# Prompt attention from transposed scores: halves stacked on partitions, V beside ones as the stationary operand, maxima from a sweep of their own

## The chip, the cores and the metric

One core of one Trainium2 chip runs the whole program in one launch. The metric is the device time in microseconds, the median of the runs.

## The reference, cut to what matters

One step of a two-layer decoder: a chunked gMLP layer, then an attention layer with forgetting (decay by cumulated log-forget values), for a prompt of 1024 tokens and for 8 single tokens with 512 cached positions each. All is computed in fp32; here only the attention of the prompt changes, per head (16 heads of 64 values) over causal pairs of query and key.

```python
logits = jnp.einsum('nqhd,nkhd->nhqk', q, k).astype(jnp.float32) * (FA_HEAD_DIM ** -0.5)
decay = jnp.swapaxes(c_q, 1, 2)[..., :, None] - jnp.swapaxes(c_k, 1, 2)[..., None, :]
causal = k_pos[None, :] <= q_pos[:, None]
logits = jnp.where(causal, logits + decay, -jnp.inf)
p = jax.nn.softmax(logits, axis=-1)
return jnp.einsum('nhqk,nkhd->nqhd', p.astype(v.dtype), v)
# then, in the mixer
return (o * jax.nn.silu(z)) @ w_out + b_out
```

## The kernel before

Each fp32 product is done as three matmuls of fp32r parts: an operand is split into a high part (rounded to fp32r) and a low part (the rest), and `three` (L1345 to L1349) accumulates low*high, high*low and high*high. Token data lie transposed: features on the partitions, tokens on the free axis.

The program has stages: the modulation, 16 V blocks, 16 pairs of Z and U blocks, 8 output blocks of the first layer, its layer norm, then the stage around the change, 8 output blocks of the attention layer (L1644 to L1676), and the tail with the decode attention and the last layer norm.

The stage around the change is a loop of 8 phases, j = 0 to 7. Phase j does the attention of heads 2j and 2j+1, and, woven in, the projections of K, Q, V and Z for pair j+1: 4 blocks (q = 0 to 3) of 16 `step`s (L1522). A step is three matmuls of 512 columns; step 0 of each block also issues the narrow group `sample_cols` (L1501), 16 matmuls of 9 columns. Phases 1 to 6 are a hardware loop of two phases per turn, phase 7 has no projections any more.

In a phase before, i runs over 16 pairs (query tile qt = i // 2, head h = i % 2). For each, TensorE does `scores` (queries on the partitions, keys on the columns, K=64 rows of one head, three matmuls per up to 512 keys, and a mask matmul on the diagonal tile), VectorE adds the decay and takes the row's maximum in one custom operation (`logits`, L1165), ScalarE takes the exponential and its sum (`exp`, L725), TensorE transposes the probabilities tile by tile (`transpose_p`, L1578), ScalarE and VectorE split them (`pt_high` L719, `pt_low` L1172), and TensorE multiplies them with V (`values`, L1588 and L1590: probabilities stationary, V moving, 128 and 64 columns). `o_part` and `o_full` divide by the sum, eight transposes (L1633) bring the result back to features on partitions, and `gate_o` (L1189) multiplies by the gate z.

Each engine has its own program, an order written out by hand; they meet at semaphores. What a phase issues and when is in `phase` of each engine. Queues: SP issues the weight loads (`load_b`), GpSimd issues the loads of the decay rows (`load_c`) and the stores of k and v (`store_kv`), and in the last phase the cache pages for the decode attention. There, VectorE also does the first 11 of 32 decode `score`s (L1140, two operations of 1024 columns each), and ScalarE and VectorE split the first two rows of the attention's result (`y2_high`, `y2_low`). K and Q of a pair are kept twice (`par`), so that the next pair is split while the current is in use.

PSUM has 8 banks: 0 and 1 for the projections, 2 and 3 (`pair(1)`) for scores, 4 and 5 (`pair(2)`) for transposes, 6 and 7 for the result of the two heads.

## Time and profile before

| | us |
|---|---|
| median of 3 runs | 2042.86 (2042.25 to 2048.98) |
| span of the profiled execution | 2045.0 (no time of its own beside the span is listed) |
| TensorE busy | 1950.4 (95%) |
| VectorE busy | 876.2 (43%) |
| ScalarE busy | 587.6 (29%) |
| GpSimd busy | 189.3 (9%) |
| mean granted TensorE clock | 0.944 |

Busy is the union of an engine's instructions. In rows of single matmuls the duration contains the pipeline's depth, so two neighbours overlap; what one costs in a dense stream is the distance between starts. PEld is TensorE's weight load, which runs beside the matmul before it. The granted clock is a share of 2.4 GHz; 0.50 is 1.2 GHz. "idle <-X" names what the engine waited for, as inferred from semaphores.

### The profile page before, as it was taken

What the parts mean: (1) busy time and instruction counts of PE and PEld (TensorE: products, weight loads), DVE (VectorE), ACT (ScalarE), POOL (GpSimd) and SP (SyncE); (2) the same over time, 40 slices, a digit from 0 to 9 for tenths busy, and PEclk for the clock granted to TensorE, in tenths of its full rate; (3) what the DMA queues carried; (4) which work ended last, traced back from release to release, by engine and by line L of the source; (5) the groups of instructions that cost most, each with busy time, mean ns of one, the idle gap of its engine ahead of it and who ended that gap; (6) DMA issues with size and microseconds to landing.
All of it is one profiled execution on the core that took longest, in us unless ns stands there. A gap on an engine that the chain in (4) does not pass through costs nothing.

```text
span 2045.0 us, 29265 instructions
## 1 busy us (share of the span) xinstructions
PE 1950.4 (95%) x11208; PEld 1685.4 (82%) x11208; DVE 876.2 (43%) x1645; ACT 587.6 (29%) x1106; POOL 189.3 (9%) x215
## 2 busy tenths in 40 slices
...
DMA packets 44071, 164.23 MB, mean 80 GB/s; under 512 B 5610, under 2 KB 6250, under 8 KB 42818
## 3 DMA queue, kind: packets, MB, share of 16 engines
q1 hardware_dynamic: 26642, 103.52, 14.4%
...
q14 instruction: 34, 0.28, 0.0%
...
## 4 chain that ended last, share of the span: by engine, by line
PE 87%; DVE 6%; issue 3%; ACT 2%; DMA 1%; POOL 0%; POOLq 0%; SPq 0%; DVEq 0%; ACTq 0%
PE bank L1347 19%; PE bank L1349 18%; PE bank L1348 18%; PE bank L1578 4%; PE bank L1588 3%; PE bank L1559 3%; PE bank L1698 3%; PE bank L1446 3%; PE bank L1504 3%; PE bank L1590 2%; PE bank L1560 2%; PE bank L1561 2%; PE bank L1435 1%; PE bank L1356 1%; PE bank L1562 1%
## 5 line engine op out<-in xcount | busy, mean ns | idle before, releaser
L1347 PE MATMUL bank<-h_hi,w_lo 128*128 128x344 f32 x1152 | 373.7, 324 | 5.7 <-DVE h_lo L859 5.0
L1348 PE MATMUL bank<-h_lo,w_hi 128*128 128x344 f32 x1152 | 368.3, 320 | 0.0
L1349 PE MATMUL bank<-h_hi,w_hi 128*128 128x344 f32 x1152 | 368.0, 319 | 0.0
L1347 PE MATMUL bank<-x_hi,w_lo 128*128 128x512 f32 x528 | 228.6, 433 | 1.8 <-DVE kqvzS L1087 1.4
L1347 PEld LDWEIGHTS bank<-h_hi,w_lo 128*128 128x128 f32 x1152 | 217.2, 189 | 11.9 <-issue 9.7
L1348 PEld LDWEIGHTS bank<-h_lo,w_hi 128*128 128x128 f32 x1152 | 217.4, 189 | 0.0
L1349 PEld LDWEIGHTS bank<-h_hi,w_hi 128*128 128x128 f32 x1152 | 217.1, 188 | 0.0
L1349 PE MATMUL bank<-x_hi,w_hi 128*128 128x512 f32 x528 | 214.2, 406 | 0.0
L1348 PE MATMUL bank<-x_lo,w_hi 128*128 128x512 f32 x528 | 214.0, 405 | 0.0
L1347 PE MATMUL bank<-y_hi,w_lo 128*128 128x344 f32 (+1 forms) x512 | 175.7, 343 | 7.2 <-ACT y_hi L605 3.1
L1348 PE MATMUL bank<-y_lo,w_hi 128*128 128x344 f32 (+1 forms) x512 | 173.6, 339 | 0.0
L1349 PE MATMUL bank<-y_hi,w_hi 128*128 128x344 f32 (+1 forms) x512 | 173.4, 339 | 0.0
L725 ACT ACTIVATE prob<-prob,nmin 128x256 f32<-128x256 f32 (+7 forms) x128 | 99.4, 777 | 240.3 <-DVE nmin L1165 240.3
L822 DVE TENSOR_TENSOR w_lo<-raw,w_hi 128x1024 fp32r<-128x1024 f32 x89 | 120.9, 1359 | 66.2 <-ACT w_hi L532 65.9
L1588 PE MATMUL bank<-Vhl,pt_hi 128*128 128x128 f32 x576 | 143.7, 308 | 3.8 <-DVE pt_lo L1172 3.8
L1172 DVE TENSOR_TENSOR pt_lo<-bank,pt_hi 128x256 fp32r<-128x256 f32 (+7 forms) x128 | 96.9, 757 | 116.4 <-ACT pt_hi L719 115.4
L1590 PE MATMUL bank<-Vhl,pt_lo 128*128 128x64 f32 x576 | 141.2, 260 | 0.0
L1588 PEld LDWEIGHTS bank<-Vhl,pt_hi 128*128 128x128 f32 x576 | 120.0, 208 | 9.1 <-DVE pt_lo L1172 4.5
L1590 PEld LDWEIGHTS bank<-Vhl,pt_lo 128*128 128x128 f32 x576 | 120.3, 209 | 4.7
L1349 PEld LDWEIGHTS bank<-x_hi,w_hi 128*128 128x128 f32 x528 | 103.7, 196 | 24.1
L1347 PEld LDWEIGHTS bank<-x_hi,w_lo 128*128 128x128 f32 x528 | 104.8, 198 | 19.3 <-DVE kqvzS L1087 1.9
L1348 PEld LDWEIGHTS bank<-x_lo,w_hi 128*128 128x128 f32 x528 | 104.1, 197 | 16.6
...
## 6 DMA issues: line engine op xcount, KB each, us to landing
raw<-units SPq DMA_DIRECT2D x105, 512.0 KB, 3.5
...
```

What stands on the lines that cost most here:

```text
L725: A(prob[:, 0:nk * P], prob[:, 0:nk * P], ACT.Exp, bias=nmin[:, i % 2:i % 2 + 1], scale=-1.0, accum_out=rsum[:, i % 2:i % 2 + 1]).then_inc ...
L822: v.tensor_tensor(w_lo[:, slot, :, :], raw[:, slot, :, :], w_hi[:, slot, :, :].bitcast(F32), ALU.subtract)\
L1172: v.tensor_tensor(pt_lo[:, 0:nk, :], pair(2)[:, 0:nk * P].rearrange("p (t c) -> p t c", c=P), pt_hi[:, 0:nk, :].bitcast(F32), ALU.subtract ...
L1347: mm(out, lhs_lo, rhs_hi, start=first, stop=False)
L1348: mm(out, lhs_hi, rhs_lo, start=False, stop=False)
L1349: return mm(out, lhs_hi, rhs_hi, start=False, stop=last)
L1446: last = mm(bank(4 + a)[0:9, TH:TH + P], scT[:, k, :], ada_ring[:, a, k, :], start=(k == 0), stop=(k == KB - 1))
L1504: last = mm(out, raw[:, slot, k, :], src[:, k, :], start=(k == 0), stop=(k == KB - 1))
L1559: mm(out, kq_lo[rows, par, 1, qs], kq_hi[rows, par, 0, ks], start=True, stop=False)
L1578: last = nc.tensor.transpose(pair(2)[:, k * P:(k + 1) * P], prob[:, k * P:(k + 1) * P], ident[:, :])
L1588: mm(out[:, 0:2 * HD], pt_hi[:, k, :], Vhl[:, k, h, :, :].rearrange("p a d -> p (a d)"), start=(k == 0), stop=False)
L1590: last = mm(out[:, 0:HD], pt_lo[:, k, :], Vhl[:, k, h, 0, :], start=False, stop=(k == nk - 1))
```

## The change

The prompt attention of a pair of heads is done the other way round:

- **Layout.** `KA` and `QA` hold, per head, 64 rows of the high part and 64 rows of the low part of K or Q on the 128 partitions; `KX` is `KA` with its halves swapped, made by four DMAs on SP's queue (`load_swapped`). One matmul with K=128 gives high*high + low*low, a second with `KX` the two mixed products. K and Q are first evacuated whole (`kf`, `qf`) by VectorE and split at the head of their phase (`kq_high` ScalarE, `kq_low` VectorE); they are no longer kept twice, and k is stored from `kf`.
- **Maxima.** `peak` computes the scores once with queries on the partitions, one matmul per up to 512 keys, and VectorE takes decay and row maximum as before, written back in place in PSUM. The maxima are rounded (`peak_round`) and `spread` brings them by matmuls against the identity to all partitions as a row over the queries; `shift` (ScalarE) copies this to `mb`.
- **Scores and probabilities.** `scores` has keys on the partitions and up to 512 queries on the columns, in 12 chunks per phase and head (`chunk`: queries in two halves, key tiles 0 to 3 and 0 to 7, cut at the diagonal). VectorE adds key decay and shift (`exponents`), ScalarE takes the exponential and its rounded copy (`probs`), GpSimd subtracts (`p_low`). No probability is transposed.
- **Values.** The stationary operand is `[V of head 0 | ones]` or `[ones | V of head 1]`, the probabilities are moving, up to 512 columns, three matmuls per chunk. The sums come out in the other 64 rows; `gate_o` is done per half of the queries with two reciprocals.
- **Order.** New orders of `phase` on all engines, phases 1 to 6 as a loop of one phase. In the last phase 8 decode scores are counted as early, six inside it and two after `y2_low`; all `y2_high` and `y2_low` come behind it. Key decays as columns (`ccol`) come from eight transposes of `fc` once, behind the first projection block. Semaphores of short sequences are merged, and several tiles move.

The diff, cut to what the text speaks of, with twelve columns less of indentation:

```diff
+def load_swapped(j):
+    sp.wait_ge(S("kq_lo"), 4 * j + 2)
...
+    for h in range(2):
+        for a in range(2):
+            sp.dma_start(KX[a * HD:(a + 1) * HD, h, :].bitcast(F32),
+                         KA[(1 - a) * HD:(2 - a) * HD, h, :].bitcast(F32)).then_inc(S("kx_in"), 16)
...
+def p_low(j, c):
+    half, kt, off, slot, diag = chunk(c)
+    for h in range(2):
+        r = (2 * c + h) % 4
+        pool.wait_ge(S("p_hi"), 24 * j + 2 * c + h + 1)
...
+        g.tensor_tensor(p_lo[:, r, off:HALF], parg[:, r, off:HALF], p_hi[:, r, off:HALF].bitcast(F32),
+                        ALU.subtract).then_inc(S("p_ready"), 1)
...
+def z_tanh(j, half):
+    act.wait_ge(S("mm"), 12 * j + half + 11)
+    if half == 0:
+        act.wait_ge(S("hbz_ready"), j + 1)
+    wait(act, S("zs_done"), 2 * j + half)
+    wait(act, S("o_done"), 2 * j + half - 1)
...
+    A(zth[:, :], bank(half), ACT.Tanh, bias=hbz2[:, 0:1], scale=0.5).then_inc(S("z_th2"), 1)
+def kq_high(j):
+    for n, (tile, src) in enumerate(((KA, kf), (QA, qf))):
+        act.wait_ge(S("evac"), 12 * j + 3 * n + 3)
+        if n == 0:
+            wait(act, S("s_done"), 24 * j)
+        for h in range(2):
+            rows = slice(h * HD, (h + 1) * HD)
+            A(tile[rows, h, :], src[rows, :], ACT.Copy).then_inc(S("kq_hi"), 1)
...
+def shift(j, half):
+    act.wait_ge(S("b_done"), 2 * j + half + 1)
+    wait(act, S("arg_ready"), 24 * j + 8 * half)
...
+    A(mb[:, :, :], ps[1][:, :, :], ACT.Copy).then_inc(S("mb_ready"), 1)
+def probs(j, c):
+    half, kt, off, slot, diag = chunk(c)
+    for h in range(2):
+        r = (2 * c + h) % 4
+        act.wait_ge(S("arg_ready"), 24 * j + 2 * c + h + 1)
...
+        A(parg[:, r, off:HALF], parg[:, r, off:HALF], ACT.Exp, scale=SCALE).then_inc(S("p_exp"), 1)
+        act.wait_ge(S("p_exp"), 24 * j + 2 * c + h + 1)
+        A(p_hi[:, r, off:HALF], parg[:, r, off:HALF], ACT.Copy).then_inc(S("p_hi"), 1)
...
+def phase(j, more):
+    kq_high(j)
+    if more:
+        split_hi(j + 1, 1)
+    shift(j, 0)
+    if more:
+        split_hi(j + 1, 2)
+    for c in range(4):
+        probs(j, c)
+    shift(j, 1)
+    if more:
+        split_hi(j + 1, 3)
+    for c in range(4, 9):
+        probs(j, c)
     if more:
         split_hi(j + 2, 0)
+    for c in range(9, 12):
+        probs(j, c)
+    if more:
+        z_tanh(j + 1, 0)
         v_hi(j + 1)
+        z_tanh(j + 1, 1)
...
+def z_evac(j, half):
+    cs = slice(half * HALF, half * HALF + HALF)
+    dve.wait_ge(S("z_th2"), 2 * j + half + 1)
...
+    v.tensor_scalar(y2T[:, j, cs], bank(half), kqvzS[:, 3, j, 8:9], 0.5, ALU.add, ALU.mult).then_inc(S("evac"), 1)
+    dve.wait_ge(S("evac"), 12 * j + half + 11)
+    v.scalar_tensor_tensor(y2T[:, j, cs], zth[:, :], 1.0, y2T[:, j, cs], ALU.add, ALU.mult)\
+        .then_inc(S("zs_done"), 1)
...
+def kq_low(j):
+    for n, (tile, src) in enumerate(((KA, kf), (QA, qf))):
+        for h in range(2):
+            rows, other = slice(h * HD, (h + 1) * HD), slice((1 - h) * HD, (2 - h) * HD)
+            dve.wait_ge(S("kq_hi"), 4 * j + 2 * n + h + 1)
...
+            v.tensor_tensor(tile[other, h, :], src[rows, :], tile[rows, h, :].bitcast(F32), ALU.subtract)\
+                .then_inc(S("kq_lo"), 1)
...
+def peak(j, qt):
+    for h in range(2):
+        dve.wait_ge(S("m_done"), 16 * j + 2 * qt + h + 1)
+        if qt == 0:
+            dve.wait_ge(S(f"ckb_in{h}"), 16 * j + 16)
...
+        out = peak_out(qt, h)
+        v.tensor_tensor_reduce(out=out, in0=out, in1=ckb[:, h, 0:(qt + 1) * P], scale=-1.0, scalar=3e38,
+                               op0=ALU.add, op1=ALU.min, accum_out=nmin[:, h, qt:qt + 1])\
+            .then_inc(S("nl_ready"), 1)
...
+def exponents(j, c):
+    half, kt, off, slot, diag = chunk(c)
+    for h in range(2):
+        r = (2 * c + h) % 4
+        dve.wait_ge(S("s_done"), 24 * j + 2 * c + h + 1)
+        wait(dve, S("pv_done"), 24 * j + 2 * c + h - 3)
+        if c in (0, 4) and h == 0:
+            dve.wait_ge(S("mb_ready"), 2 * j + half + 1)
+        if c == 0 and h == 0:
+            dve.wait_ge(S("cph_in"), j + 1)
...
+        v.scalar_tensor_tensor(parg[:, r, off:HALF], ps[1 + slot][:, h, off:HALF], cph[:, h, kt:kt + 1],
+                               mb[:, h, off:HALF], ALU.add, ALU.add).then_inc(S("arg_ready"), 1)
+def gate_o(j, half, more):
+    cs = slice(half * HALF, half * HALF + HALF)
+    dve.wait_ge(S("pv_done"), 24 * j + 8 + 16 * half)
+    dve.wait_ge(S("zs_done"), 2 * j + (3 if half == 1 and more else 2))
+    wait(dve, S("o_done"), 2 * j + half)
+    v.reciprocal(rc[0:HD, :], bank(6)[HD:P, :]).then_inc(S("o_nrm"), 1)
+    v.reciprocal(rc[HD:P, :], bank(7)[0:HD, :]).then_inc(S("o_nrm"), 1)
+    dve.wait_ge(S("o_nrm"), 6 * j + 3 * half + 2)
+    v.tensor_tensor(rc[:, :], rc[:, :], y2T[:, j, cs], ALU.mult).then_inc(S("o_nrm"), 1)
+    dve.wait_ge(S("o_nrm"), 6 * j + 3 * half + 3)
+    v.tensor_tensor(y2T[0:HD, j, cs], bank(6)[0:HD, :], rc[0:HD, :], ALU.mult)
+    v.tensor_tensor(y2T[HD:P, j, cs], bank(7)[HD:P, :], rc[HD:P, :], ALU.mult).then_inc(S("o_done"), 1)
...
+def phase(j, more):
+    kq_low(j)
+    key_decay(j)
     if more:
+        evac_s(j + 1, 0)
+    peak(j, 0)
+    peak(j, 1)
+    if more:
+        evac_kqv(j + 1, 0, 0)
+        split_lo(j + 1, 1)
+    else:
+        tok(1, qtok1, 0)
+    peak(j, 2)
+    peak(j, 3)
+    peak_round(j, 0)
+    peak(j, 4)
+    peak(j, 5)
+    if more:
+        evac_kqv(j + 1, 0, 1)
+        evac_s(j + 1, 1)
+    peak(j, 6)
+    peak(j, 7)
+    peak_round(j, 1)
+    if more:
+        split_lo(j + 1, 2)
+    exponents(j, 0)
+    exponents(j, 1)
+    if more:
+        evac_kqv(j + 1, 1, 0)
+    exponents(j, 2)
+    exponents(j, 3)
+    if more:
+        evac_kqv(j + 1, 1, 1)
+        evac_s(j + 1, 2)
+    exponents(j, 4)
+    if more:
+        split_lo(j + 1, 3)
+    gate_o(j, 0, more)
+    exponents(j, 5)
+    if more:
+        evac_kqv(j + 1, 2, 0)
+    for c in range(6, 9):
+        exponents(j, c)
+        if not more:
+            score(c - 6)
+    if more:
+        evac_kqv(j + 1, 2, 1)
         evac_s(j + 1, 3)
+    exponents(j, 9)
+    if more:
         split_lo(j + 2, 0)
+    else:
+        score(3)
+    exponents(j, 10)
+    if not more:
+        score(4)
+    exponents(j, 11)
+    if more:
+        z_evac(j + 1, 0)
+    else:
+        score(5)
+    gate_o(j, 1, more)
+    if more:
         v_lo(j + 1)
+        z_evac(j + 1, 1)
...
+def peak(j, qt):
     qs = slice(qt * P, (qt + 1) * P)
+    if qt == 0:
+        pe.wait_ge(S("kq_lo"), 4 * j + 4)
+        wait(pe, S("arg_ready"), 24 * j)
+    if qt == 1:
+        pe.wait_ge(S("v_hl"), j + 1)
+    if 2 <= qt < 4:
+        pe.wait_ge(S("nl_ready"), 16 * j + 2 * qt - 2)
+    for h in range(2):
+        if qt == 4:
+            pe.wait_ge(S("nl_ready"), 16 * j + 8) if h == 0 else pe.wait_ge(S("mb_ready"), 2 * j + 1)
+        if qt > 4:
+            pe.wait_ge(S("nl_ready"), 16 * j + 2 * qt + h - 1)
+        out = peak_out(qt, h)
+        for k in range(0, (qt + 1) * P, HALF):
+            ks = slice(k, min(k + HALF, (qt + 1) * P))
+            mm(out[:, ks], QA[:, h, qs], KA[:, h, ks], start=True, stop=ks.stop < (qt + 1) * P)
+        mm(out[:, qs], identb[:, :], maskb[:, :], start=False, stop=True).then_inc(S("m_done"), 1)
+def spread(j, half):
+    pe.wait_ge(S("nr_ready"), 2 * j + half + 1)
+    if half == 1:
+        pe.wait_ge(S("arg_ready"), 24 * j + 6)
+    for h in range(2):
+        for t in range(4):
+            i = 4 * half + t
+            last = mm(ps[1][:, h, t * P:(t + 1) * P], nminr[:, h, i:i + 1].broadcast_to([P, P]), identr[:, :],
+                      start=True, stop=True)
+    last.then_inc(S("b_done"), 1)
+def scores(j, c):
+    half, kt, off, slot, diag = chunk(c)
+    ks, qs = slice(kt * P, (kt + 1) * P), slice(half * HALF + off, half * HALF + HALF)
+    if c == 0:
+        pe.wait_ge(S("kx_in"), 64 * j + 64)
+        pe.wait_ge(S("nl_ready"), 16 * j + 16)
+    elif c == 1:
+        pe.wait_ge(S("nl_ready"), 16 * j + 15)
+    elif c == 5:
+        pe.wait_ge(S("mb_ready"), 2 * j + 2)
+    else:
+        pe.wait_ge(S("arg_ready"), 24 * j + 2 * c - (0 if c == 4 else 2))
+    for h in range(2):
+        out = ps[1 + slot][:, h, off:HALF]
+        mm(out, KA[:, h, ks], QA[:, h, qs], start=True, stop=False)
+        last = mm(out, KX[:, h, ks], QA[:, h, qs], start=False, stop=not diag)
+        if diag:
+            last = mm(out[:, 0:P], maskb[:, :], identb[:, :], start=False, stop=True)
+        last.then_inc(S("s_done"), 1)
+def values(j, c):
+    half, kt, off, slot, diag = chunk(c)
+    end = c in (3, 11)
+    if c == 0:
+        pe.wait_ge(S("v_hl"), j + 1)
+        wait(pe, S("o_done"), 2 * j)
+    if c == 4:
+        pe.wait_ge(S("o_done"), 2 * j + 1)
+    for h in range(2):
+        r = (2 * c + h) % 4
+        pe.wait_ge(S("p_ready"), 24 * j + 2 * c + h + 1)
+        out = bank(6 + h)[:, off:HALF]
+        mm(out, v_block(0, kt, h), p_hi[:, r, off:HALF], start=kt == 0, stop=False)
+        mm(out, v_block(0, kt, h), p_lo[:, r, off:HALF], start=False, stop=False)
+        mm(out, v_block(1, kt, h), p_hi[:, r, off:HALF], start=False, stop=end).then_inc(S("pv_done"), 1)
...
+    steps(0, 7)
+    peak(j, 0)
+    peak(j, 1)
+    if not more:
+        pe.wait_ge(S("evac"), 12 * KB)
+        turn(1, 0)
+    steps(7, 9)
+    peak(j, 2)
+    peak(j, 3)
+    steps(9, 12)
+    spread(j, 0)
+    peak(j, 4)
+    steps(12, 14)
+    peak(j, 5)
+    steps(14, 16)
+    peak(j, 6)
+    steps(16, 18)
+    peak(j, 7)
+    steps(18, 21)
+    scores(j, 0)
+    steps(21, 23)
+    scores(j, 1)
+    steps(23, 24)
+    values(j, 0)
+    steps(24, 26)
+    scores(j, 2)
+    steps(26, 27)
+    values(j, 1)
+    steps(27, 29)
+    scores(j, 3)
+    steps(29, 31)
+    values(j, 2)
+    steps(31, 32)
+    spread(j, 1)
+    steps(32, 33)
+    scores(j, 4)
+    steps(33, 35)
+    values(j, 3)
+    steps(35, 37)
+    scores(j, 5)
+    steps(37, 39)
+    values(j, 4)
+    steps(39, 40)
+    for c in range(6, 11):
+        scores(j, c)
+        steps(3 * c + 22, 3 * c + 24)
+        values(j, c - 1)
+        steps(3 * c + 24, 3 * c + 25)
+    scores(j, 11)
+    steps(55, 57)
+    values(j, 10)
+    steps(57, 60)
+    values(j, 11)
+    steps(60, 61)
     if more:
         transpose_vt(j + 1)
+    steps(61, 64)
...
```

## Rows read from the trace of the kernel before

**Rows 1.** The page's part 4: the chain that ended last, share of the span by engine.
```profile
PE 87%; DVE 6%; issue 3%; ACT 2%; DMA 1%; POOL 0%; POOLq 0%; SPq 0%; DVEq 0%; ACTq 0%
```

**Rows 2.** Windows: stretch, length, busy (count) of PE, PEld, DVE, ACT, POOL; clock, DMA, GB/s.
```profile
1142.00:1240.00 98.00, 97.94 (x577) 81.61 (x576) 45.73 (x115) 39.95 (x89) 4.57 (x5) 0.98 0.13 44
...
1746.00:1840.00 94.00, 84.61 (x328) 68.72 (x328) 60.57 (x108) 30.52 (x67) 20.70 (x38) 0.53 0.37 125
1840.00:1945.00 105.00, 98.64 (x460) 79.50 (x458) 85.18 (x90) 27.61 (x32) 23.74 (x44) 0.98 0.55 199
```

**Rows 3.** Chain in order of time, narrow groups: start us, us, what.
```profile
1004.95 1.69 PE bank L1504 x16
1017.82 1.69 PE bank L1504 x16
...
1044.91 1.74 PE bank L1504 x16
...
1647.84 1.74 PE bank L1504 x16
```

**Rows 4.** Timeline of TensorE in a phase: start us, us, line, operation.
```profile
1153.24 0.28 PE L1560 MATMUL bank<-kq_lo,kq_hi 64*128 64x256 f32 x1
1153.36 0.28 PE L1561 MATMUL bank<-kq_hi 64*128 64x256 f32 x1
...
1156.98 0.33 PE L1561 MATMUL bank<-kq_hi 64*128 64x384 f32 x1
...
1157.28 0.47 PE L1347 MATMUL bank<-x_hi,w_lo 128*128 128x512 f32 x1
1157.60 0.39 PE L1348 MATMUL bank<-x_lo,w_hi 128*128 128x512 f32 x1
1157.83 0.40 PE L1349 MATMUL bank<-x_hi,w_hi 128*128 128x512 f32 x1
```

**Rows 5.** Timeline of TensorE: first of 16 value matmuls, first step behind.
```profile
1733.45 0.22 PE L1588 MATMUL bank<-Vhl,pt_hi 128*128 128x128 f32 x1
...
1735.15 0.48 PE L1347 MATMUL bank<-x_hi,w_lo 128*128 128x512 f32 x1
```

**Rows 6.** Groups of VectorE, shapes apart: count, busy us, mean ns, idle before.
```profile
L1151 DVE TENSOR_REDUCE scol<-pages 128x16 f32<-128x1024 f32 x32 | 39.0, 1220 | 1.1
...
L1120 DVE SCALAR_TENSOR_TENSOR y2T<-zth,zb 128x512 f32<-128x512 f32 x4 | 2.8, 692 | 0.1
L843 DVE COPY m<-bank 9x512 f32<-9x512 f32 x4 | 2.7, 679 | 34.0 <-PE bank L1356 34.0
L1023 DVE RECIPROCAL lr<-lr 128x1 f32<-128x1 f32 x16 | 2.6, 164 | 7.2 <-ACT lr L638 7.2
L1020 DVE TENSOR_SCALAR lr<-lmv 128x1 f32<-128x1 f32 x16 | 2.5, 154 | 0.6
...
L920 DVE RECIPROCAL rsd<-rsd 128x8 f32<-128x8 f32 x3 | 0.6, 203 | 0.8 <-ACT rsd L578 0.8
...
L918 DVE TENSOR_SCALAR rsd<-bank 128x8 f32<-128x8 f32 x3 | 0.5, 167 | 1.9 <-PE bank L1412 1.9
```

**Rows 7.** Groups of ScalarE and GpSimd, the same columns.
```profile
L719 ACT ACTIVATE pt_hi<-bank 128x512 fp32r<-128x512 f32 x16 | 9.6, 598 | 4.1 <-PE bank L1578 3.5
...
L747 ACT ACTIVATE y_hi<-y2T 128x1024 fp32r<-128x1024 f32 x8 | 7.9, 1045 | 3.6 <-DVE y2T L1189 3.6
...
L443 POOL TENSOR_TENSOR kf<-kq_hi,kq_lo 128x1024 f32<-128x1024 f32 x8 | 19.0, 2373 | 274.6 <-DVE kq_lo L1108 274.6
```

**Rows 8.** Windows of 6 us behind a narrow group in the third phase.
```profile
1264.00:1270.00 6.00, 6.00 (x17) 4.21 (x18) 1.09 (x5) 0.49 (x1) 2.95 (x2) 0.50 0.50 179
1270.00:1276.00 6.00, 6.00 (x25) 4.54 (x24) 1.47 (x4) 2.67 (x5) 0.00 (x0) 0.70 0.00 0
```

**Rows 9.** Timeline of TensorE: the last step; k=7 of the first output block.
```profile
1744.98 0.39 PE L1349 MATMUL bank<-x_hi,w_hi 128*128 128x512 f32 x1
...
1848.38 0.49 PE L1347 MATMUL bank<-y_hi,w_lo 128*128 128x512 f32 x1
```

More of the change, by code:

```diff
@@ L460, in phase @@
                     load_c(j + 1, h)
-            phase(0, 0)
-            with pool.Fori(0, KB // 2 - 1) as i2:
-                phase(2 * i2 + 1, 1)
-                phase(2 * i2 + 2, 0)
+                store_k(j + 1)
+                for c in range(12):
+                    p_low(j, c)
+                store_v(j + 1)
+            phase(0)
+            with pool.Fori(1, KB - 1) as j:
+                phase(j)
             pool.wait_ge(S("evac"), 12 * KB)
@@ L749, in phase @@
[L749 to L767 removed]
+                act.wait_ge(S("o_done"), 2 * k + 2)
@@ L778, in _ @@
-            phase(KB - 1, 1, False)
-            act.wait_ge(S("y2_ready"), KB)
-            act.wait_ge(S("s_done"), 16 * KB)
-            act.wait_ge(S("kf_ready"), KB)
-            for k in range(2, KB):
+                    z_tanh(j + 1, 1)
+            phase(0, True)
+            with act.Fori(1, KB - 1) as j:
+                phase(j, True)
+            phase(KB - 1, False)
+            act.wait_ge(S("k_out"), 16 * KB)
+            act.wait_ge(S("kq_lo"), 4 * KB)
+            act.wait_ge(S("kx_in"), 64 * KB)
@@ L785, in _ @@
+            act.wait_ge(S("s_done"), 24 * KB)
+            for k in range(KB):
                 y2_high(k)
@@ L1105, in evac_lo @@
                     return
[L1106 removed]
+                wait(dve, S("kq_lo"), 4 * j)
                 if q == 0:
[L1108 to L1121 removed]
@@ new lines, in _ @@
+            split_lo(0, 1)
+            evac_s(0, 0)
+            evac_kqv(0, 0, 0)
+            evac_kqv(0, 0, 1)
+            dve.wait_ge(S("cc_mm"), 1)
+            link(v.tensor_copy(ccol[:, :, :], bank(6)[:, 0:TT * H].rearrange("p (t h) -> p h t", h=H)))
+            split_lo(0, 2)
+            evac_s(0, 1)
+            evac_kqv(0, 1, 0)
+            evac_kqv(0, 1, 1)
+            split_lo(0, 3)
+            evac_s(0, 2)
+            evac_kqv(0, 2, 0)
+            evac_kqv(0, 2, 1)
+            split_lo(1, 0)
@@ L1239, in _ @@
             gates(1, "fa_b_out")
-            for k in range(2, KB):
+            for k in range(KB):
                 y2_low(k)
+            for n in range(6, EARLY):
+                score(n)
             def new_key():
@@ L1597, in _ @@
                     step(0, q, n)
-            transpose_vt(0)
-            def phase(j, par, more):
-                for i in range(16):
-                    if i >= 1:
-                        transpose_p(j, i - 1)
-                    scores(j, i, par)
-                    before = -(3 * i) % 16
-                    first = before if more and 0 < before < 3 else 3
-                    if more:
-                        for n in range(3 * i, 3 * i + first):
-                            step(j + 1, n // 16, n % 16)
-                    if i >= 1:
-                        values(j, i - 1)
-                    if more:
-                        for n in range(3 * i + first, 3 * i + 3):
-                            step(j + 1, n // 16, n % 16)
-                    if not more and i == 0:
-                        pe.wait_ge(S("evac"), 12 * KB)
-                        turn(1, 0)
-                def z_steps(a, b):
+                if q == 0:
+                    pe.wait_ge(S("f_step"), 4)
+                    for t in range(TT):
+                        last = nc.tensor.transpose(bank(6)[:, t * H:(t + 1) * H], fc[:, t * P:(t + 1) * P], ident[0:H, 0:H])
+                    last.then_inc(S("cc_mm"), 1)
@@ L1620, in z_steps, with phase, steps @@
+                if q == 2:
+                    pe.wait_ge(S("v_sides"), 2)
+            transpose_vt(0)
+            def phase(j, more):
+                def steps(a, b):
                     for n in range(a, b):
                         if more:
-                            step(j + 1, 3, n)
-                transpose_p(j, 15)
-                z_steps(0, 4)
-                values(j, 15)
-                z_steps(4, 8)
+                            step(j + 1, n // 16, n % 16)
+                steps(0, 7)
[52 more added lines that the diff above has]
+                steps(60, 61)
@@ L1641, in _ @@
-            phase(KB - 1, 1, False)
+                steps(61, 64)
+            phase(0, True)
+            with pe.Fori(1, KB - 1) as j:
+                phase(j, True)
+            phase(KB - 1, False)
             for b in range(KB):
```

443 lines of the change are left out of this document (154 added, 289 removed).

## Prediction

> **What bounds the kernel now.** First the chain of waits: TensorE carries 87% of it [rows 1], so only what lengthens or shortens TensorE's line of work counts, unless an engine behind it makes it stop. Then the windows: in an ordinary phase of the attention loop TensorE is busy for all 98.0 us, while VectorE works 45.7 and ScalarE 40.0 us; in the last phase, which has no projection steps left to weave in, TensorE runs at a granted clock of 0.53 and all engines wait in turn [rows 2]. The chain in order of time gives the lengths: a projection block of 16 steps with its 16 narrow matmuls takes 12.87 us, and six phases take 602.9 us, 100.5 each, so seven take 703.4 [rows 3]. The change touches the seven phases, the last one, and the two ends of the block after it.
>
> **TensorE's work in a phase.** Start to start, a 512-column matmul takes 0.23 us, a 256-column one 0.12 (a 128-column one no less, I take it), a 384-column one 0.17 between them; with its mask matmul the 384-column one takes 0.30, 0.13 more, and the first matmul behind a mask 0.32 instead of 0.23, so a mask costs 0.22 [rows 4]. One pass over the causal half for both heads is 12 matmuls of 512, 4 of 384, 8 of 256 or 128: 12*0.23 + 4*0.17 + 8*0.12 = 4.4 us. Small matmuls and transposes come at 16 in 1.70 us, 0.106 each [rows 5].
> Before: 4 blocks 51.5; three score passes 13.2; 16 masks 3.5; 72 transposes 7.6 and 144 value matmuls 15.3; 16 transposes 1.7. Sum 92.8; the window has 98.0, so changes between kinds of work cost 5.2.
> After: blocks 51.5; peaks one pass 4.4; two score passes 8.8 (hi and lo stacked, K=128 instead of 64, which I take as free: columns set the time in the rows); 32 masks 7.0; values three passes 13.2; spread 16 matmuls 1.7 (estimate 2.0 with its changes); transposes of V 0.9. Sum 87.8, plus changes of kind, of which I take 1.3 above what the list already holds (between 0 and 5.2): 89.1. So TensorE's own work falls by 9 us per phase, 62 over seven. If nothing else happened, that were the gain.
>
> **What the other engines now put in front of TensorE.** The new step with no row of its own size is gate_o: per half, two reciprocals of 512 columns, one product in SBUF and two out of PSUM. VectorE's time doesn't depend on partitions (9 x 512 takes 0.68, 128 x 512 takes 0.69 us [rows 6]), so 64 rows cost as much as 128. The reciprocal: 164 ns for one column, 203 for eight; an ordinary operation has 154 and 167 [rows 6]. The slope is (203-164)/7 = 5.6 ns per column, or, if the one-column row is mostly the fixed 154, 7.0. An ordinary slope is about 1.1. So 512 columns cost 0.16+511*5.6 ns = 3.0 us, or 3.7; I take 3.3. The far bound below is that the eight-column row misleads and it costs 0.69 like the others. A half of gate_o is then 2*3.3 + 0.69 + 2*0.69 + hops of 0.05 to 0.1 = 8.9 us (3.7 at the far bound).
> The Trainium skill (VectorE: DVE Perf Modes, "First, the fixed hardware budget") says that Reciprocal runs as an iterative divide with a repeat count of 8. The trace agrees that it is far above the ordinary slope (5.6 to 7.0 against 1.1 ns); taken as eight cycles a column it would be an estimated 4.3 us each and some 30 us more in all than my sum.
>
> Who waits for it, in one phase, t = 0 at the end of values(j,11):
> - *Second half of gate_o.* It ends at 8.9. Queued behind it on VectorE are v_lo (1.22 like the 1024-column rows) and z_evac(j+1,1); z_tanh(j+1,1) on ScalarE waits for it too, since zth and rc are one tile. The first operation of z_evac, which frees bank 1, ends at 8.9+1.3+0.8 = 11.1. TensorE has one step 0.7, transposes 0.9, three steps 2.1 and the narrow group 1.7, and stands at step(j+2,0,0) from 5.5. **Stall 5.6.** At the far bound 0.4.
> - *Splitting K and Q*, now at the head of the phase and single-buffered: ScalarE's four copies of 1.05 [rows 7] begin after z_tanh, VectorE's four subtractions of 1.22 [rows 6] after z_evac at 11.9 and end at 16.9; seven steps bring TensorE to 15.9. **Stall 1.0.** KX's four transfers start at 14.4 and aren't needed before some 41; even several times the usual few us would be hidden.
> - *Before spread(0)* VectorE must do peaks 0 to 3 (8 operations), evac_kqv and a scaled split: 8 us against TensorE's 6: **1.9**. The second peak 4 waits for ScalarE's copy of the spread (1.05): **0.8**. Peak 7 behind peak 6 (1.1 each): **0.7**.
> - *values(j,0)* follows scores(j,0) by 3.2 us, and the chain exponents 0.7, exp and copy 0.6 each, GpSimd's subtraction 1.2 (half of 2.37 [rows 7]), for two heads in turn, takes 4.7: **0.9** after the first head's work. Later chunks have 5.8 us before their values and hide it; GpSimd's 2.4 us per chunk lie under TensorE's 4.5.
> - *First half of gate_o* starts 1.5 after values(3), behind exponents(4) and the split of z's weights; values(4) needs its banks. TensorE has two steps, scores(5), two steps, 3.7. **Stall 1.5+8.9-3.7 = 6.7.** At the far bound 1.5.
> Sum of stalls 17.6. The clock: behind a narrow group the trace shows the granted clock at 0.50 for 6 us and at 0.70 over the next 6 [rows 8], about 10 us at 1.2 instead of 2.4 GHz, where each matmul of 512 columns takes twice its time; the two long stalls invite it. I take 3 us of it behind each, between none and these 10, which costs 1.5; one of these is partly inside the K and Q wait: 2 per phase (0 to 9, the upper end if each drop lasts 10 us). The phase is 89.1+17.6+2.0 = 108.7 us against 100.5. Phase 0 starts without a gate_o before it: -4.5. Seven phases: 7*108.7-4.5 = 756.4 against 703.4, **+53.0**.
>
> **The last phase.** Before, from the last step (1745.0) to k=7 of the first output block (1848.4) are 103.4 us [rows 9]. After, the same chain by hand: gate_o and the splits to 13 (from the last step), eight peaks one by one with the turn of q and both copies to 32, chunks 0 to 3 to 49, gate_o to 58, chunks 4 to 11 at half clock (a 512-column chunk 10*0.43 = 4.4) to 85, gate_o to 94, then eight y2_low of 1.22 in a row to 104. That is **+1** (-10 at the far bound, -6 more if the denser matmuls are granted the full clock). The transposes and sixteen small chains that go are paid back by gate_o and by y2_low, of which none lies inside the phase any more.
> **The output blocks.** EARLY 11 becomes 8, and of these 8 two come after y2_low: 26 scores of 2.44 (two rows of 1.22) instead of 21 lie beside these blocks. VectorE had 85 of 105 us filled [rows 2]; with 12 us more and a run of seven double scores (6.2 us against TensorE's 5.6) it delays three weight splits by about 1: **+3**. **Head:** eight transposes of fc behind the first block: **+0.9**. Moving evacuations from ScalarE to VectorE is free under the blocks.
>
> **Sum.** 2045.0 + 53.0 + 1 + 3 + 0.9 = 2103 for the profiled execution, whose span lies 2.1 above the median of the runs; I know nothing of what lies around the span, so take that difference: 2101, rounded to **2100**.
>
> **Rivals.**
> - *A, the forecast*, reciprocals of 3.0 to 3.7: 2080 to 2125. The repeatable 39 ns between one and eight columns speak for it. Chance 0.57.
> - *B, the reciprocal runs at the ordinary rate.* Stalls per phase 0.4+1.0+3.4+0.9+1.5 = 7.2, no clock loss: 96.3, seven phases less the 1 that phase 0 saves 673, -30; last phase -10; +3.9: 2007, range 1985 to 2025. For it: no row has more than eight columns. Against it: both rows fit only with a steep slope. 0.17.
> - *C, steep reciprocals but cheap rest*: the small stalls vanish under slack that I don't see, no clock loss: 108.7-2.0-4.4 = 102.3, seven phases +8, the last at better clock -6: 2050. It decides against a clear loss if the waits b, spread and peak 7 are all absent. 0.10.
> - *D, the clock*: every long stall is followed by a low stage of 10 us as in [rows 8], 5 each instead of 1.5, once more per phase +3.5, seven times +25; with a reciprocal at the upper slope (0.4 more, four per phase and one in the last, +15) 2140. 2125 to 2145. 0.10.
> - *E, the change doesn't do what it says*: GpSimd's subtraction, slowed by VectorE's use of SBUF, becomes the pace of the chunks (over 4.5 us for two of 512 columns; it was 2.4). At 5 it adds 0.5 on each of six chunks, 3 per phase, 2125. The rows show 2.37 beside a busy VectorE, so 0.06.
>
> **How the numbers follow.** Likeliest 2100, its own range 2080 to 2125. The range for 8 in 10 goes down to 2010, which takes in C and about half of B, and up to 2140: outside are half of B and some of D and E. A measurement tells 0.3%, 6 us, from no change. Faster: B and a quarter of C, 0.20; same (2037 to 2049) 0.05; slower 0.75.
>
> **What would show it.** The row RECIPROCAL 64 x 512: 3.0 to 3.7 us, or 0.7 and B. TensorE idle before values(4) by about 6.7 and before the first full matmul of the next phase by 5.6, released by VectorE at y2T. Ordinary phases of 107 to 110 us with TensorE busy about 90. The last phase near 100. If TensorE's idle time lies elsewhere, or a phase is below 100, the forecast is wrong in its mechanism; if phases of 108 stand without long reciprocals, in its reason.

## The result, and the profile after

The changed kernel takes 2118.09 us (median of 4 runs, 2113.36 to 2118.48) against 2043.24 us before (4 runs, 2042.25 to 2048.98): ratio 1.0351, 95% interval 1.0329 to 1.0374. It is 3.5% slower; 2100 was forecast, in a range of 2010 to 2140. The span of the profiled execution is 2117.0 us against 2045.0, the mean granted clock 0.930 against 0.944.

The page of the changed kernel, parts 1 and 4 (busy time, share of the span, instructions; then the chain that ended last by engine):
```profile
PE 1869.0 (88%) x10256; PEld 1592.4 (75%) x10256; DVE 1041.0 (49%) x1583; ACT 580.4 (27%) x994; POOL 365.2 (17%) x401
...
PE 73%; DVE 17%; issue 5%; ACT 3%; POOL 1%; DMA 0%; DVEq 0%; SPq 0%; ACTq 0%; POOLq 0%
```
TensorE works 81 us less than before, and its share of the chain falls from 87% [rows 1] to 73%; VectorE's rises from 6% to 17%. The stretches that answer to [rows 2], an ordinary phase, the last one and the output blocks (length; busy of PE, PEld, DVE, ACT, POOL; granted clock, DMA, GB/s):
```profile
1270.00:1377.50 107.50, 91.45 (x455) 73.40 (x453) 64.03 (x105) 36.29 (x73) 26.38 (x28) 0.91 0.16 49
1818.00:1912.00 94.00, 58.35 (x226) 40.48 (x226) 71.64 (x96) 35.58 (x61) 38.55 (x50) 0.70 0.35 107
1912.00:2010.00 98.00, 90.08 (x411) 71.37 (x410) 84.47 (x83) 17.83 (x21) 28.02 (x52) 0.98 0.64 223
```
The first window ends inside a wait. From narrow group to narrow group the phases are of two kinds in turn, 111.3 and 107.4 us:
```profile
1182.51:1293.83 111.32, 93.52 (x459) 75.01 (x458) 66.95 (x107) 39.09 (x76) 26.35 (x28) 0.88 0.16 48
1293.83:1401.18 107.35, 89.17 (x458) 71.84 (x457) 66.67 (x107) 39.12 (x76) 26.38 (x28) 0.94 0.16 49
```
Both have the same matmuls, and the same waits to 0.4 us; they differ by the granted clock. TensorE stands still for 18 us of a phase, where the window before had 0.1. The waits of TensorE in the whole program say for whom (total us, times, longest):
```profile
PE bank L1734 <- DVE y2T L1266: 70.4, 8, 9.3
PE bank L1470 <- DVE y2T L1167: 36.1, 7, 5.8
...
PE bank L1696 <- DVE nminr L1232: 13.6, 8, 2.4
PE bank L1685 <- DVE QA L1186: 13.2, 1, 13.2
PE bank L1470 <- DVE y_lo L1193: 11.3, 4, 10.8
PE bank L1734 <- POOL p_lo L486: 10.7, 25, 1.3
```
L1734 behind L1266 is values(4) behind gate_o: 8.8 us in the mean, 9.3 in the last phase. L1470 behind L1167 is the first projection step of the next phase behind z_evac: 5.8 in an ordinary phase, 1.5 in phase 0, which has no gate_o ahead of it. L1696 is spread, 1.6 in an ordinary phase. VectorE around the first half of gate_o (start us, us):
```profile
1322.08 4.29 DVE L871 SCALAR_TENSOR_TENSOR w_lo<-raw,one_p,w_hi 128x128 fp32r<-128x128 f32 x8
1326.40 3.36 DVE L1260 RECIPROCAL rc<-bank 64x512 f32<-64x512 f32 x1
1329.80 3.35 DVE L1261 RECIPROCAL rc<-bank 64x512 f32<-64x512 f32 x1
1333.30 0.69 DVE L1263 TENSOR_TENSOR rc<-rc,y2T 128x512 f32<-128x512 f32 x1
1334.02 0.68 DVE L1265 TENSOR_TENSOR y2T<-bank,rc 64x512 f32 x1
1334.72 0.69 DVE L1266 TENSOR_TENSOR y2T<-bank,rc 64x512 f32 x1
```
The half takes 9.0 us, and a weight split of 4.3 us stands ahead of it.

Where the 72 us between the two spans are, by landmarks that both kernels have (the first transpose of vT, the two rows of [rows 9] and the first matmul on pages): ahead of the loop +2.1; seven phases, to the last projection step, 763.0 against 701.8, +61.3; from the last step to k=7 of the first output block 105.3 against 103.4, +1.9; from there to the pages 108.7 against 102.0, +6.7; behind that nothing.

### The profile page after: what moved, and what is told of

Its sections match the earlier page's. It is cut to its first block, busy times and chain, and to the rows that moved or that the text cites. A ratio compares the mean times of both kernels' runs of the same rounds, so it can differ in the third digit from the quotient of the medians.

```text
span 2117.0 us, 27900 instructions
## 1 busy us (share of the span) xinstructions
PE 1869.0 (88%) x10256; PEld 1592.4 (75%) x10256; DVE 1041.0 (49%) x1583; ACT 580.4 (27%) x994; POOL 365.2 (17%) x401
## 4 chain that ended last, share of the span: by engine, by line
PE 73%; DVE 17%; issue 5%; ACT 3%; POOL 1%; DMA 0%; DVEq 0%; SPq 0%; ACTq 0%; POOLq 0%
PE bank L1470 17%; PE bank L1471 16%; PE bank L1472 16%; PE bank L1883 3%; PE bank L1569 3%; DVE rc L1261 3%; PE bank L1627 2%; DVE w_lo L871 2%; PE bank L1734 2%; PE bank L1685 2%; DVE rc L1260 2%; PE bank L1736 2%; PE bank L1735 2%; DVE bank L1226 1%; PE bank L1479 1%
## 5 line engine op out<-in xcount | busy, mean ns | idle before, releaser
L1470 PE MATMUL bank<-h_hi,w_lo 128*128 128x344 f32 x1152 | 373.5, 324 | 4.9 <-DVE h_lo L902 4.3
L1470 PE MATMUL bank<-x_hi,w_lo 128*128 128x512 f32 x528 | 232.2, 440 | 37.7 <-DVE y2T L1167 36.1
L486 POOL TENSOR_TENSOR p_lo<-parg,p_hi 128x512 fp32r<-128x512 f32 (+1 forms) x192 | 193.9, 1026 | 308.8 <-ACT p_hi L781 307.4
L1470 PEld LDWEIGHTS bank<-h_hi,w_lo 128*128 128x128 f32 x1152 | 217.1, 188 | 11.2 <-issue 8.6
L1470 PE MATMUL bank<-y_hi,w_lo 128*128 128x344 f32 (+1 forms) x512 | 175.7, 343 | 18.5 <-DVE y_lo L1193 11.3
L1251 DVE SCALAR_TENSOR_TENSOR parg<-bank,cph,mb 128x512 f32<-128x512 f32 (+1 forms) x192 | 110.6, 613 | 156.2 <-PE bank L1718 119.6
L779 ACT ACTIVATE parg<-parg 128x512 f32<-128x512 f32 (+1 forms) x192 | 99.0, 516 | 314.9 <-DVE parg L1251 314.9
L1470 PEld LDWEIGHTS bank<-x_hi,w_lo 128*128 128x128 f32 x528 | 108.6, 206 | 56.4 <-DVE y2T L1167 36.7
L1734 PE MATMUL bank<-p_hi,Vst 128*128 128x512 f32 (+1 forms) x192 | 74.5, 388 | 81.4 <-DVE y2T L1266 70.4
L580 ACT ACTIVATE w_hi<-raw 128x1024 fp32r<-128x1024 f32 x89 | 94.4, 1061 | 127.1 <-PE bank L1472 121.4
L434 POOL TENSOR_TENSOR vcur<-V,vr 128x1024 f32<-128x1024 f32 x16 | 33.0, 2063 | 550.5 <-PE bank L1558 327.7
```

Of the source, the lines that this page charges most:

```text
L486: g.tensor_tensor(p_lo[:, r, off:HALF], parg[:, r, off:HALF], p_hi[:, r, off:HALF].bitcast(F32), ALU.subtract).then_inc(S("p_ready"), 1)
L580: A(w_hi[:, slot, :, :], raw[:, slot, :, :], ACT.Copy).then_inc(S("hi_ready"), 1)
L779: A(parg[:, r, off:HALF], parg[:, r, off:HALF], ACT.Exp, scale=SCALE).then_inc(S("p_exp"), 1)
L1251: v.scalar_tensor_tensor(parg[:, r, off:HALF], ps[1 + slot][:, h, off:HALF], cph[:, h, kt:kt + 1], mb[:, h, off:HALF], ALU.add, ALU.add).t ...
L1470: mm(out, lhs_lo, rhs_hi, start=first, stop=False)
L1734: mm(out, v_block(0, kt, h), p_hi[:, r, off:HALF], start=kt == 0, stop=False)
```

## The experiments

All start from the changed kernel and were timed beside the kernel before on the same chip (2042 to 2049 there). For the seven phases of the changed kernels I compare one stretch in all traces, from the first transpose of vT for phase 0 to the last one for phase 7: 761.1 us after. (The kernel before has 695.6, but there these transposes stand 6.2 us ahead of the last projection step, in the others 1.9; against it the landmarks of the section above hold.)

**e1: no division.** The two reciprocals become copies.
```diff
-v.reciprocal(rc[0:HD, :], bank(6)[HD:P, :])
-v.reciprocal(rc[HD:P, :], bank(7)[0:HD, :])
+v.tensor_copy(rc[0:HD, :], bank(6)[HD:P, :])
+v.tensor_copy(rc[HD:P, :], bank(7)[0:HD, :])
```


> Both reciprocals of each half of gate_o become copies of the same 64 x 512 elements, so the division is left out of the output; every wait, the order and all other work stay. A copy of that shape from PSUM should take about 0.7 us (the 64 x 512 product L1265 took 0.68), so a half of gate_o falls from 9.0 to about 3.7 us. Theory 1 (the length of the two reciprocals is what costs): the wait of values(4) falls from 8.8 to about 3.5 us, the wait for z_evac from 5.2 to under 1, the half-clock stretches behind both go for the most part, a phase falls from 109.3 to about 99 us, the last phase by about 10: 2118 - 72 - 10 = about 2035, range 2025 to 2050. Rival (the order of VectorE's queue and the clock cost as much as the reciprocals do, and the freed time is taken by the next wait): only 4 to 5 us of a phase come back, about 2085.

Measured 2019.44 us, ratio to before 0.9894 (0.9875 to 0.9913). Its VectorE group and its waits of TensorE:
```profile
L1260 DVE COPY rc<-bank 64x512 f32<-64x512 f32 x16 | 11.1, 694 | 7.1 <-PE bank L1736 6.8
```
```profile
PE bank L1734 <- DVE y2T L1266: 27.1, 8, 4.5
...
PE bank L1470 <- DVE y2T L1167: 4.1, 7, 1.5
```
The seven phases take 677.9 us, 83 less, and the last one loses 15. The length of the reciprocals is the loss: without it the same order is 1% faster than the kernel before. The gain is even 16 us above the forecast and the time below its range; the wait for K and Q in the last phase shrinks too (13.2 to at most 7.9), which is a part of it.

**e2: the split behind the gate.**
```diff
 exponents(j, 4)
-split_lo(j + 1, 3)
 gate_o(j, 0, more)
 exponents(j, 5)
 evac_kqv(j + 1, 2, 0)
+split_lo(j + 1, 3)
```


> split_lo(j+1,3) goes from ahead of gate_o(j,0) to behind gate_o(j,0), exponents(5) and evac_kqv(2,0). Theory (the gate starts late because of the 4.3 us split in front of it): the gate starts right behind exponents(4), some 4 us earlier, bounded by the end of values(3); the wait of values(4) falls from 8.8 to about 5, and each of seven phases by 3.8 us or a little more by the clock: about 2118 - 27 = 2091, range 2085 to 2098. Rival (the split is only moved, and now holds up the exponents behind it): the split is then 2 to 4 us ahead of exponents(6), whose chunk values(6) wants, and the gain is halved or gone: 2105 to 2118.

Measured 2096.89 us (2094.6 to 2097.42), ratio 1.027 (1.0249 to 1.029): 21 us faster than the changed kernel. The wait of values(4), line numbers one lower here:
```profile
PE bank L1733 <- DVE y2T L1266: 47.2, 8, 9.2
```
5.9 each, and a phase is 3.3 shorter. Of the 27 us expected 21 come: the order did cost.

**e3: GpSimd later.** Its subtraction for chunk 4 waits for the end of the scaled split.
```diff
+if c == 4:   # not in the last phase
+    pool.wait_ge(S("lo_ready"), U_B + 4 * j + 8)
```


> GpSimd's subtraction for chunk 4 waits until VectorE's scaled split (split_lo(j+1,3)) is done; nothing else changes, and values(4) is waiting for gate_o by then in any case. Theory (the split takes 4.3 us instead of 2.1 because GpSimd's 128 x 512 subtractions run beside it): the eight instructions of L871 take 2.1 to 2.2 us together there, the gate starts 2.1 us earlier, the wait of values(4) falls from 8.8 to 6.7, as forecast, and seven phases give 15 us or a little more: about 2102, range 2097 to 2107. Rival (the split is slow by itself in that place, by its source or by ScalarE beside it): L871 keeps 4.3 us, no change, 2118.

Measured 2112.38 us (2110.07 to 2115.84), above the range of 2097 to 2107. The median is 6 us less, but the ratio to before, 1.0345 (1.0324 to 1.0367), can't be told from the changed kernel's 1.0351. VectorE at the same place, and the wait (line numbers are 2 higher here):
```profile
1323.03 2.18 DVE L873 SCALAR_TENSOR_TENSOR w_lo<-raw,one_p,w_hi 128x128 fp32r<-128x128 f32 x8
1325.24 3.36 DVE L1262 RECIPROCAL rc<-bank 64x512 f32<-64x512 f32 x1
```
```profile
PE bank L1736 <- DVE y2T L1268: 55.7, 8, 9.2
```
So the split's 4.3 us were GpSimd's doing: 2.2 without it, and the waits fall by 14.7 us as expected. But the time didn't follow. The seven phases of after and of e3:
```profile
1045.30:1806.40 761.10, 640.87 (x3192) 515.26 (x3191) 459.86 (x745) 273.50 (x525) 184.71 (x196) 0.90 0.16 48
```
```profile
1046.50:1806.20 759.70, 655.30 (x3192) 525.36 (x3191) 446.27 (x745) 273.45 (x525) 183.82 (x196) 0.89 0.16 49
```
The same 3192 matmuls are busy for 14.4 us longer. It is not that a shorter wait alone has a longer low stretch behind it. The first value matmul behind the wait and the first one at full speed again, twice in the changed kernel, then in e3:
```profile
1224.21 0.79 PE L1734 MATMUL bank<-p_hi,Vst 128*128 128x512 f32 x1 [8.84 <-DVE y2T L1266]
1229.80 0.40 PE L1470 MATMUL bank<-x_hi,w_lo 128*128 128x512 f32 x1
...
1335.54 0.79 PE L1734 MATMUL bank<-p_hi,Vst 128*128 128x512 f32 x1 [8.84 <-DVE y2T L1266]
1339.01 0.39 PE L1472 MATMUL bank<-x_hi,w_hi 128*128 128x512 f32 x1
```
```profile
1334.39 0.79 PE L1736 MATMUL bank<-p_hi,Vst 128*128 128x512 f32 x1 [6.73 <-DVE y2T L1268]
1339.97 0.40 PE L1472 MATMUL bank<-x_hi,w_lo 128*128 128x512 f32 x1
```
Matmuls stood 0.43 apart, half clock, for 5.3 us and for 3.4 us behind the same wait of 8.84, and for 5.3 behind e3's 6.73. The changed kernel's phase of 111.3 us also has a stretch of half clock at the next spread(0) (1283.6 to 1291.1) that its phase of 107.4 lacks. In e3 phases 2 to 6 are all alike, 109.2 to 109.4 us with TensorE busy 93.5 to 93.7, as in the changed kernel's longer kind: 2 us shorter than that one, 2 longer than the other. So the shorter wait came through only in every second phase. Why the low stretches come in every phase there and are fewer in every second one here, no run shows.

**e4: one reciprocal of 128 rows.** ScalarE first copies both sums into rc.
```diff
+A(rc[0:HD, :], bank(6)[HD:P, :], ACT.Copy)
+A(rc[HD:P, :], bank(7)[0:HD, :], ACT.Copy)
-v.reciprocal(rc[0:HD, :], bank(6)[HD:P, :])
-v.reciprocal(rc[HD:P, :], bank(7)[0:HD, :])
+v.reciprocal(rc[:, :], rc[:, :])
```


> ScalarE copies the two sums out of PSUM into rc (2 x 64 x 512, about 0.6 us each), and VectorE divides once on 128 x 512 in place of twice on 64 x 512. Theory (a reciprocal costs by its columns, whatever the number of partitions): one of 128 x 512 takes 3.3 to 3.4 us, and a half of gate_o falls from 9.0 to 5.6; for half 1 ScalarE's 1.3 us stands ahead of it, for half 0 it is hidden behind the 4.3 us split. The wait of values(4) falls by 3.4, the wait for z_evac by about 2.1, the last phase by 5, and the clock gives back 0 to 2 us a phase: 2118 - 7 x 5.5 - 5 = about 2074, range 2062 to 2082. Rival (it costs by elements): the one reciprocal takes 6.7 us and the copies come on top, 2118 to 2130.

```profile
L1275 DVE RECIPROCAL rc<-rc 128x512 f32<-128x512 f32 x16 | 53.6, 3348 | 22.4 <-ACT rc L772 22.4
```
128 rows take 3.35 us as 64 did: columns alone count. Measured 2086.65 us (2074.39 to 2089.04), ratio 1.0226 (1.0204 to 1.0247). The profiled execution is the 2074.39 one, at a granted clock of 0.938; the others had 0.931 to 0.934. In it the two waits are 5.7 and 3.5 us, where 5.4 and 3.1 were expected. The median is 13 us above the forecast and outside its range (2062 to 2082); the recorded clocks point at the clock, but the slower executions have no trace, so this is not shown.

**e6: TensorE kept busy while it waits** (the clock by itself).
```diff
+def fill(j, slot, done, n):
+    pe.wait_ge(S("arg_ready"), 24 * j + done)
+    for i in range(n):
+        mm(ps[slot][:, i % 2, :], identr[:, :], over(identr[:, :], 4))
```


> The changed kernel with matmuls added that nobody reads (identr against identr read four times, 512 columns each, into a free PSUM bank): 32 of them, 7.4 us at 0.23 us each, in the wait of values(4) in seven phases, and 20, 4.6 us, in the wait for z_evac; every wait and all other work stay. Both waits are longer than the added work (8.8 and 5.2 us). Theory (the low clock behind a stall is a price of its own: in the run with the later subtraction the waits fell by 14.7 us and TensorE's busy time for the same matmuls rose by 14.4): the half-clock stretches behind both waits go. The real matmuls of the seven phases then take some 20 us less than the 641 us of after, the changed kernel is 15 to 25 us faster with 90 us of useless work in it: about 2098, range 2090 to 2105. Rival (the clock has its dips anyway, or the waits are what counts): no change or slower, 2115 to 2125.

Measured 2101.57 us (2096.94 to 2108.95), ratio 1.0294 (1.0259 to 1.0329). Seven phases:
```profile
1044.60:1786.50 741.90, 694.82 (x3537) 560.78 (x3535) 459.38 (x745) 273.69 (x525) 184.41 (x196) 0.97 0.16 50
```
The 364 useless matmuls, 84 us of work at 0.23 each, make the kernel 16 us faster: the granted clock rises from 0.90 to 0.97 and a phase falls by 2.7 us. That is what filling these two waits gives back of the clock's cost.

**e2 and e4 together** (with ScalarE's copies ahead of probs(4)):
```diff
 exponents(j, 4)
-split_lo(j + 1, 3)
 gate_o(j, 0, more)        # with the one reciprocal
```


> The edits of the runs with the split behind the gate and with one reciprocal of 128 x 512 together, and ScalarE copies the sums of half 0 ahead of probs(4) and not behind it, so that they are ready about 1.3 us after values(3) ends. Theory (the time is the sum of the waits that gate_o leaves on TensorE): gate_o(j,0) then ends 1.3 + 3.4 + 2.1 = 6.8 us after values(3), where it ended 12.6 after it: the wait of values(4) falls from 8.8 to about 3; the wait for z_evac stays at the 3.5 of one reciprocal. Seven phases at about 100.5 and a last one 5 to 6 us shorter: 2118 - 57 - 6 = 2055, range 2045 to 2068. Rival (shortened waits come back as TensorE running longer at the low clock, as in the run with the later subtraction, where 14.7 us of wait gave 5 us of time): half of that, about 2080.

Measured 2069.04 us (2066.8 to 2071.93), ratio 1.0095 (1.006 to 1.013). The two waits:
```profile
PE bank L1747 <- DVE y2T L1280: 32.5, 8, 6.4
PE bank L1483 <- DVE y2T L1180: 24.7, 7, 3.9
```
That is 4.1 and 3.5 each, for 3 and 3.5 forecast: 1 us a phase too small, some 8 of the 14 us that the time lies above its forecast of 2055 (range to 2068). The rest stays open. Shortening the gate and starting it earlier doesn't reach the kernel before.

**f: both gates out of TensorE's way.**
```diff
 exponents(j, 4)
+keep(j)              # values of half 0: PSUM to vT; ScalarE: sums to rc
 exponents(j, 5)
 split_lo(j + 1, 3)
-gate_o(j, 0, more)
 exponents(j, 6)
+recip(j, 0, 0)       # 128 x 256
 exponents(j, 7)
+recip(j, 0, 1)
+gate_o(j, 0)         # two products from SBUF
 evac_kqv(j + 1, 2, 0)
...
 z_evac(j + 1, 0)
-gate_o(j, 1, more)   # now in the peak sweep of phase j + 1
 v_lo(j + 1)
 z_evac(j + 1, 1)
```


> No wait of TensorE hangs on the reciprocals any more. Half 0: VectorE copies the two blocks of values out of PSUM (into the free half of vT, in the last phase into kf) and ScalarE the two blocks of sums (into rc); values(4) waits for these copies alone, and the division (two pieces of 128 x 256) and two products from SBUF stand between the exponents of chunks 5 to 8. Half 1: the gate of phase j is done in the peak sweep of phase j+1, where VectorE idles (2.4 and 2.6 us ahead of the peaks of rows 4 and 5), with z_tanh, v_lo, z_evac and the K and Q splits ahead of it; rc still shares its place with zth. Theory (the change loses by these waits alone, its TensorE work being less than before): a phase has 91.4 us of TensorE work, 1.7 for the spread, about 1.5 for z_evac, 0 to 0.5 at values(4) and 1 for the clock, about 96; seven give 761 - 672 = 89 less than after, the last phase 8 to 10 less: about 2020, range 2010 to 2030, below the kernel before (2042). Rival (VectorE's queue is full enough that the pieces delay peaks and exponents, and the wait moves to them): phases of 100 to 103, 2048 to 2070.

Measured **2002.46 us** (1997.44 to 2002.79), ratio to before 0.9774 (0.9741 to 0.9807), 116 us less than the changed kernel, and 8 us below its range of 2010 to 2030. Seven phases, and VectorE in the place of the first half's gate:
```profile
1044.20:1687.80 643.60, 611.42 (x3193) 493.36 (x3191) 426.62 (x751) 289.09 (x551) 187.72 (x196) 0.98 0.18 57
```
```profile
1287.92 4.29 DVE L885 SCALAR_TENSOR_TENSOR w_lo<-raw,one_p,w_hi 128x128 fp32r<-128x128 f32 x8
1292.13 1.40 DVE L1266 SCALAR_TENSOR_TENSOR parg<-bank,cph,mb 128x512 f32<-128x512 f32 x2
1293.45 1.74 DVE L1285 RECIPROCAL rc<-rc 128x256 f32<-128x256 f32 x1
1295.22 1.41 DVE L1266 SCALAR_TENSOR_TENSOR parg<-bank,cph,mb 128x512 f32<-128x512 f32 x2
1296.54 1.74 DVE L1285 RECIPROCAL rc<-rc 128x256 f32<-128x256 f32 x1
1298.43 1.08 DVE L1291 TENSOR_TENSOR rc<-rc,y2T 128x512 f32<-128x512 f32 x1
1299.54 1.67 DVE L1296 TENSOR_TENSOR y2T<-vT,rc 128x512 f32 x1
```
A phase takes 91.9 us, where 96 was forecast, with the division still 3.5 us a half. To the last projection step the seven take 645.5 us against 701.8 before the change, 8.0 less a phase. TensorE's time for the same matmuls is 29.5 us below the changed kernel's, as its clock is 0.98. TensorE's own work was put 4 us too high in this forecast (91.4 from the trace of the changed kernel, which contains the low clock; it is 87.3 here). The last phase missed the other way: 103.5 us from the last transposes of vT to the last y2_low, where the changed kernel has 105.9 and 96 to 98 was forecast.

**f2: the scores of the last phase spread out.**
```diff
 exponents(j, 5)
+score(0)
...
 exponents(j, 8)
-score(0); score(1); score(2)
+score(1)
```


> As the run with both gates moved, with the scores of the last phase placed elsewhere: one behind exponents(5), (8), (9), (10) and (11) each, in place of three in a row behind exponents(8), and the sixth goes from between gate_o(7,1) and y2_low to behind y2_low. Theory (the last phase gained only 2.4 us of the 8 to 10 forecast because three scores, 8.2 us of VectorE, stood ahead of exponents(9), for which values(9) waited 6.3 us, and a sixth one stood ahead of y2_low): the 6.3 us wait goes, y2_low starts 2.4 us earlier beside that, and the last phase falls from 103.5 to about 95, with up to 2.4 us given back in the output blocks: 2002 - 6 = 1996, range 1991 to 2000. Rival (VectorE is full in that stretch in any order, 77 us of 103): the wait only moves, 2000 to 2004.

Measured **1997.32 us** (1990.26 to 1999.18), ratio to before 0.9758 (0.9719 to 0.9796), the best version. The last phase takes 95.0 us; the wait for GpSimd behind the late exponents went from 6.3 to at most 2.3 us. Of the 8.5 us the output blocks take 4.1 back (114.1 us from the last y2_low to the pages, 110.0 in f).

**e7: fewer elements in the scores of the output blocks.**
```diff
-v.tensor_tensor(pages[:, b % 2, p, :], pages[:, b % 2, p, :], qbs[b % 2][:, :], ALU.mult)
+v.tensor_tensor(pages[:, b % 2, p, 0:w], ...)   # w = 64 for the second score of a half block
```


> In the output blocks, each second score of a half block (nine of them) multiplies 64 columns of its page instead of 1024, so those scores are wrong in the output; the reduction over 1024 columns stays. VectorE loses nine times about 1.15 us there, 10 us. Theory (the output blocks are paced by VectorE since the change left more scores to them: 108.7 us from k = 7 of the first block to the first matmul on pages, 102.0 before): that stretch falls to TensorE's own pace, by 5 to 8 us: 2118 - 6 = 2112. Rival (the stretch is longer by something else, such as the transfers of weights and pages): it keeps 108 to 109 us, 2117 to 2118.

Measured 2114.85 us (2110.04 to 2115.84): within 0.3% of the changed kernel, so the time alone decides nothing. In the trace the stretch from the last y2_low to the pages is 106.3 us against 110.0. Ten us less on VectorE give 3.7, for 5 to 8 forecast: VectorE is the pace of part of these blocks. The other 3 us over the kernel before stay open.

## Why the prediction was right, and where its terms were off

**TensorE's own work, 89.1 forecast: 2 too high.** In f, nearly at full clock (0.98), it is busy 611.4/7 = 87.3 us a phase.

**The reciprocal, 3.3 forecast: right.** 3.36 and 3.35 us for 512 columns, from two rows of one and eight columns [rows 6]: 6.3 ns a column above the fixed 0.15. The half of gate_o took 9.0 for 8.9. Rival B had the right outcome for its own world: e1, with copies of 0.69, runs in 2019 us, inside B's 1985 to 2025. The Trainium skill (VectorE: DVE Perf Modes, "First, the fixed hardware budget") gives the reciprocal a repeat count of 8; eight cycles a column would be an estimated 4.3 us. The trace has 3.35, and 1.74 for 256 columns, and decides.

**The waits, 17.6 forecast, about 18 measured, in another mixture.** In an ordinary phase z_evac is 5.8 for 5.6; spread 1.6 for 1.9; the shift 0.6 for 0.8; values(0) and later chunks behind GpSimd 0.7 for 0.9; peaks 0.4 for 0.7; K and Q 0 for 1.0, as the projection steps ahead of them run at half clock and cover it. **values(4) 8.8 for 6.7 is the term that was mis-sized**: the prediction let the gate start 1.5 us behind values(3), with a split of 2.1 us; it took 4.3 and the gate started 3.4 behind, beside GpSimd's subtraction, which the kernel before did not have. The group of all these splits, 36.1 us in the kernel before:
```profile
L871 DVE SCALAR_TENSOR_TENSOR w_lo<-raw,one_p,w_hi 128x128 fp32r<-128x128 f32 x128 | 49.6, 458 | 1.8 <-ACT w_hi L588 1.8
```
e3 shows that this was the cause. It also shows that its 15 us are not the gap: taken away, 6 come back at most. That the sum of the waits is right is in part luck: this 2.1 too little is made up for by the smaller ones that were put too high. Rival E saw the two engines meet the other way round: GpSimd's subtraction of 512 columns took 1.3 us in the changed kernel for 1.2 forecast, and it was VectorE's split that grew.

**The clock, 2.0 forecast, about 4 measured.** TensorE is busy 91.6 us in a phase for what f does in 87.3: about 2 in every second phase, as forecast, and about 6 in the others, near rival D's 5.5. With the waits: 87.3 + 18 + 4 = 109.3, the mean of six phases (1074.90 to 1730.84 in the chain, 109.3 each), for 108.7 forecast. Two errors met here, own work 2 too high and clock 2 too low, and that they cancel is luck. Rival D was right in its mechanism (e6 gets 2.7 of the 4 back) and too large in price in the mean; by its own counts its 15 us for the upper slope are 12 to 13. Rival C's condition, that the small waits are absent, didn't hold: spread, shift and peaks are there with 2.6 us.

**The rest.** Seven phases +61.3 for +53.0: 3.7 are the 0.6 us in each of six, 2.9 are phase 0, which took 107.1 for 104.2, and 1.7 the baseline, 701.8 for 703.4. Last phase +1.9 for +1. Output blocks +6.7 for +3: the seven double scores were priced at three weight splits late by 1 us each; in the chain there the scores now have 33% and the three matmul lines of the blocks 31%, where the kernel before had 5% and 71%:
```profile
1920.07 1.15 DVE pages L1209
1921.24 1.22 DVE scol L1212
1922.46 1.14 DVE pages L1209
1923.63 1.22 DVE scol L1212
...
1929.14 0.99 issue
1930.14 1.21 DVE w_lo L865
```
Two scores, then (behind two more) the next block's weight split: e7 confirms 3.7 of the 6.7. The head +2.1 for +0.9. Last, the span was taken to lie 2 us above the median and lies 1 below: 3 us. Of the 18 us between 2100 and 2118, 8 are the phases, 4 the output blocks, 3 the span, 2 the head and the last phase, 1 the rounding to 2100.
